# Another order of the slots of an expert's block over the partitions

## What is computed

```python
def hier_moe(h, p):
    """h (N, D): top-1 expert group, then top-2 experts inside it; experts are SwiGLU MLPs."""
    ...
    order = jnp.argsort(e_assign)
    e_s, tok_s, w_s = e_assign[order], tok_assign[order], w_assign[order]
    ...
    buf = jnp.zeros((n_blocks * EXPERT_BLOCK, D_MODEL), h.dtype).at[dest].set(h[tok_s])
    ...
    def expert_block(args):
        xb, e = args
        return (jax.nn.silu(xb @ p['w_exp_gate'][e]) * (xb @ p['w_exp_up'][e])) @ p['w_exp_down'][e]

    out = lax.map(expert_block, (buf.reshape(n_blocks, EXPERT_BLOCK, D_MODEL), block_expert))
    out = out.reshape(-1, D_MODEL)
    return jnp.zeros((n, D_MODEL), h.dtype).at[tok_s].add(out[dest] * w_s[:, None].astype(h.dtype))
```

## Time and profile before

| what | value |
|---|---|
| median of three timed executions | 1260.64 us |
| the profiled execution, its own time | 1264.99 us |
| its span, first to last instruction | 1263.3 us |
| TensorE busy in the span | 1041.9 us (82%) |
| VectorE, ScalarE, GpSimd busy | 410.2, 328.0, 251.9 us |
| weights of the experts | 192 pieces of 1 MB |
| gathers and scatters of 4 KB rows | 34 gathers, 32 scatters |
| stretch with the DMA engines at or above 0.9 | slices 25 to 38 of 40, 758 to 1200 us |

### The profile page before, as it was taken

How to read it: one execution, slowest core, us unless ns; L and a number is a source line. 1 busy time by engine, 2 the same in 40 slices (tenths; PEclk the granted TensorE clock), 3 DMA queues, 4 the chain that set the end, 5 groups by cost and what they waited for, 6 DMA issues and landing times.

```text
span 1263.3 us, 17373 instructions
## 1 busy us (share of the span) xinstructions
PE 1041.9 (82%) x6707; PEld 662.2 (52%) x6707; DVE 410.2 (32%) x917; ACT 328.0 (26%) x666; POOL 251.9 (20%) x551
## 2 busy tenths in 40 slices
PE   5999999779987776989999589987877788888870
PEld 5999999656665553767644333333332333333320
DVE  4346536646844443422413520100000000000006
ACT  6432221445642222120011112322222122211222
POOL 0005960388832110000000001111110111111010
PEclk9999999887978887989999679999899999998895
DMA  8322334331017542770220869999999999999956
GB/s 341 138 68 70 108 120 163 104 149 34 2 38 255 181 134 90 315 275 1 76 123 17 322 254 402 390 401 415 403 405 398 406 402 403 405 407 410 405 228 229
DMA packets 74993, 299.64 MB, mean 237 GB/s; under 512 B 12471, under 2 KB 34871, under 8 KB 48407
## 3 DMA queue, kind: packets, MB, share of 16 engines
q1 hardware_dynamic: 65854, 279.89, 57.5%
q0 software_dynamic: 7904, 17.59, 4.3%
q10 hardware_dynamic: 1152, 1.05, 0.3%
HBM read 284.26 MB, written 25.05 MB: 245 GB/s over the span
## 4 chain that ended last, share of the span: by engine, by line
DMA 27%; PE 25%; DVE 3%; issue 2%; SPq 2%; ACT 1%; POOL 0%; POOLq 0%
DMA local_tail<-in_w_exp 14%; DMA arena<-in_w_exp 11%; PE ps L2199 6%; PE ps L1779 5%; PE ps L1739 3%; PE ps L1700 3%; PE ps L1749 2%; PE ps L2216 2%; SPq L2108 1%; PE ps L2186 1%; PE ps L1716 1%; DVE arena L2358 1%; PE ps L1711 1%; SPq L2113 1%; DMA arena<-scratch_h,arena 1%
## 5 line engine op out<-in xcount | busy, mean ns | idle before, releaser
L352 PE MATMUL ps<-local_project 128*128 128x288 f32 (+4 forms) x1608 | 207.2, 291 | 15.3 <-DVE local_project L490 11.6
L2199 PE MATMUL ps<-arena,local_tail 128*64 128x512 f32 x760 | 196.7, 607 | 27.7 <-DMA arena<-in_w_exp 20.3
L352 PEld LDWEIGHTS ps<-local_project 128*128 128x128 f32 (+1 forms) x1608 | 205.8, 185 | 16.3 <-DVE local_project L391 11.5
L2301 DVE SCALAR_TENSOR_TENSOR local_tail<-arena,ps 64x512 f32<-64x512 f32 x32 | 21.7, 679 | 427.4 <-ACT arena L2267 427.4
L2199 PEld LDWEIGHTS ps<-arena,local_tail 128*64 128x64 f32 x760 | 63.2, 139 | 133.7 <-issue 132.1
L2216 PE MATMUL ps<-arena 128*64 128x512 f32 x256 | 89.3, 679 | 32.4 <-DMA arena<-in_w_exp 15.6
L2144 POOL DMA_INDIRECT scratch_rows<-local_tail,arena x32 | 29.5, 922 | 394.3 <-ACT local_tail L2275 393.2
L2216 PE MATMUL ps<-local_tail,arena 128*64 128x512 f32 x256 | 89.6, 681 | 16.1 <-DMA local_tail<-in_w_exp 16.1
L2199 PE MATMUL ps<-local_tail 128*64 128x512 f32 x264 | 80.1, 596 | 5.3 <-DMA local_tail<-in_w_exp 4.2
L2275 ACT ACTIVATE local_tail<-ps 64x512 f32<-64x512 f32 x64 | 37.9, 593 | 148.4 <-PE ps L2216 147.6
L2216 PEld LDWEIGHTS ps<-arena 128*64 128x64 f32 x256 | 26.4, 155 | 76.9 <-issue 73.5
(11 more groups left out here) (401 smaller groups left out, 1505.7 us busy)
## 6 DMA issues: line engine op xcount, KB each, us to landing
arena<-in_w_exp SPq DMA_DIRECT2D x127, 1024.0 KB, 29.0
local_tail<-in_w_exp SPq DMA_DIRECT2D x65, 1024.0 KB, 29.4
arena<-in_w_rest SPq DMA_DIRECT2D x9, 1024.0 KB, 5.6
local_attention<-in_cache SPq DMA_DIRECT2D x56, 128.0 KB, 2.7
arena<-in_w_wide SPq DMA_DIRECT2D x6, 1040.0 KB, 4.9
arena<-scratch_sig SPq DMA_DIRECT2D x2, 2304.0 KB, 13.4
arena<-in_x SPq DMA_DIRECT2D x2, 2048.0 KB, 11.7
arena<-in_cache SPq DMA_DIRECT2D x32, 128.0 KB, 2.2
```

The source lines that it names most:

```text
L352: mm = pe.matmul(out, stationary(s, k), moving(m, k), start=k == 0 and a == 0, stop=k == KD - 1 and a == 2)
L2199: mm = pe.matmul(c.ps[SLOTS * u:SLOTS * (u + 1), BANKS[q][u], :], XT[:, 4 * half + k], c.sets[s][2 * half + u][:, k], start=half == 0 and ...
```

## The change

One constant is made in another way. Before, slot (partition) p took the token of rank p. Now partition p takes the token of rank 16 (p mod 4) + p / 4 (whole division). Partitions 0 to 7 so hold ranks 0, 16, 32, 48, 1, 17, 33, 49. The constant feeds the table and the short way of the first two blocks alike, so gathers, products and scatters agree. No instruction is added, removed or moved on any engine: each engine's list of instructions is the same in both kernels. What differs is which partitions hold a token when fewer than 64 do.

```diff
@@ -119,7 +119,7 @@
     c["valid"][:] = np.arange(TILES) * P + r[:, None] < TOK
     c["blkno"][:] = np.arange(BLOCKS)
     c["blkslot"][:] = SLOTS * np.arange(TABLE + 1)
-    c["slot"][:] = np.arange(SLOTS) - SLOTS
+    c["slot"][:] = np.arange(SLOTS) % 4 * 16 + np.arange(SLOTS) // 4 - SLOTS
 
     token = np.arange(TILES)[None, None, :, None] * P + r[:, None, None, None]
```

## The result

The changed kernel takes 1275.11 us in the median of four timed executions (1272.44 to 1276.52), the kernel before, timed beside it, 1261.41 us. The ratio is **1.0091, with a 95% interval of 1.0058 to 1.0123**: slower, by 13.7 us in the medians, by 11.5 us in the ratio, and by 7 to 16 us within its interval. Forecast were 22.4 us. The profiled execution of after took 1272.44 us with a span of 1270.7 us, 7.45 us more than the profiled execution before.

What follows compares the result with a forecast made beforehand. The weight stream bounds the kernel from about 820 us, its end set by the last DMA engine. Terms 21.8 + 0.3 + 0.3 = 22.4 us, on the median of 1260.64 us, gave 1283.0 us, range 1270 to 1289 us.

Steps and rivals of the forecast that it cites:

- So I take engine = partition mod 16: Gathers and scatters: rows are dealt one to each of 16 DMA engines, then again, read from the last scatter's rounds.
- The count of rows: Rows beside the weight stream: the worst engine goes from 165 to 240, 75 rows more.
- The price of a row: Time one 4 KB row adds to its DMA engine beside the weights: 0.29 us, with ends 0.16 and 0.33.
- the taper: End of the weight stream before: the share falls evenly, last engine 17 us after the first, read as 56 rows' difference.
- the main term: Worst DMA engine's extra rows delay the last weight landing: 75 x 0.29 = 21.8 us (12.0 to 24.8).
- The two small terms: First gather gets a fourth row on its worst engine, last scatter a fourth round: 0.3 us each.
- The forecast's cover for the other scatters: Scatters land in 11.5 us against 16 us for a block; a fourth row's 0.3 us is hidden by waiting for weights.
- The other signs: Profile after: two blocks take 33.9 to 34.5 us, GB/s falls to about 385 and the DMA share below 1.
- The second step, to 0.25 or less: End of the weight stream: after a step to some 0.5, the share drops to 0.25 or less and holds to the end.
- It levels the engines: Rival: dealing is by neighbouring partitions, so the new order evens the engines; 7 us earlier, 1253.6 us; chance 0.05.
- nothing moves: Rival: dealing turns between groups of 16 partitions, worst engine 159 rows before and after; 1260.6 us; chance 0.05.
- The bare price: Rival: a row beside the weights costs only 0.16 us, sum 12.0 + 0.5, 1273 us (1270 to 1277); chance 0.18.

Runs made afterwards that it cites:

- ranks dealt over pairs: Kernel before, with partition p holding rank 16 (2 (p / 32) + p mod 2) + (p / 2) mod 16: 1256.06 us, ratio 0.9958.
- offsets: Kernel before, with each expert from the third on starting at another slot, 5e mod 16, and two more VectorE instructions: 1260.29 us, ratio 0.9992.
- both halves: Kernel before, reordered so each round of 16 ranks lies in 32 partitions, not 16 neighbouring ones: 1261.87 us, ratio 1.0001.
- pairs, offsets: Kernel with ranks dealt over pairs, plus another starting slot (5e mod 16) for each expert from the third on: 1256.54 us, ratio 0.9956.
- both halves, offsets: Kernel with rounds of 16 ranks spread over 32 partitions, plus another starting slot for each expert from the third on: 1258.55 us, ratio 0.9969.
- one engine: Kernel before, with only ranks 32 and 48 exchanged for ranks 14 and 15, loading one engine by partition mod 16: 1267.85 us, ratio 1.0041.
- groups exchanged: Kernel before, with the second and third group of 16 ranks changing places: 1274.7 us, ratio 1.0113.

## Why the prediction was right and where it failed

**Right: the bound and the sign.** The last DMA engine sets the end of the weight stream, the new order gives eight engines nearly all rows, and the stream ends later. The step to a share of 0.5 at 1216 us is the sign that was named for it. Everything ahead of the experts stayed. In part this was luck: the new order splits the engines eight and eight by partition mod 16 (206 to 240 rows against 2 to 95) and by pairs (217 to 234 against 26 to 65) alike, so the sign and the step came out though the dealing was wrong. The time lies in the stated range, 1270 to 1289 us, but in the part that the forecast gave to a rival (1270 to 1277 us): the width of the range holds it, not the working behind 1283 us.

**The step that failed: "So I take engine = partition mod 16".** It was read from the rounds of the lone scatter, taken as 16, 16 and 5 rows. These rounds exclude groups of four neighbours, the one dealing by neighbours that I held against them. But the last five were read from one window of 0.5 us, and that window hides two rounds. Cut finer, in the kernel before:

```profile
1232.90:1233.00 0.10, 0.00 (x0) 0.00 (x0) 0.00 (x0) 0.00 (x0) 0.00 (x0) 0.50 0.27 41
1233.00:1233.10 0.10, 0.00 (x0) 0.00 (x0) 0.00 (x0) 0.00 (x0) 0.00 (x0) 0.50 0.33 42
1233.10:1233.20 0.10, 0.00 (x0) 0.00 (x0) 0.00 (x0) 0.00 (x0) 0.00 (x0) 0.50 0.02 0
1233.20:1233.40 0.20, 0.00 (x0) 0.00 (x0) 0.00 (x0) 0.00 (x0) 0.00 (x0) 0.50 0.18 41
```

That is one row, one row, a gap, and two more rows. With 33 rows ahead of them, the rounds are 16, 16, 3 and 2. By partition mod 16 no engine has a fourth row. By pairs partitions 32 to 36 lie on three engines that have two rows already: two of them get a third and a fourth row and one a third, which is 16, 16, 3 and 2. So the trace of before already told the two dealings apart; the joined window didn't. The second support, that 165 down to 109 rows fit an even taper, doesn't tell them apart either: by pairs the engines have 192, 180, 171, 163, 160, 150, 138 and so on down to 88, even too. The Trainium skill, "DMA: Bandwidth & Descriptors", section "The descriptor swizzle", gives an engine four neighbouring partitions and the four that lie 32 further on, for a transfer to 128 partitions. The measured rule for these DMAs of 64 has the same form with two in place of four. The prediction took the page's groups of four as the only form of neighbours, and so put aside with them what was nearly right.

**The count of rows.** By pairs the fullest engine goes from 192 to 234 rows, 42 more, not 75 (165 to 240).

**The price of a row.** 0.29 us was the taper of 17 us over 56 rows. By pairs there are 104 rows between the first engine and the last, and 17 / 104 = 0.16 us, the bound from below: the time that 4.1 KB takes at 25.6 GB/s. Other orders say the same: in the trace the sixteen landings of the last weight piece lie 17.1 us apart in before, 9.6 us with ranks dealt over pairs, 8.8 us with offsets and 7.9 us with both halves. By pairs that is over 104, 56, 46 and 46 rows, 0.16 to 0.19 us a row; by partition mod 16 it would be over 56, 82, 10 and 56. (Levelled further, 19 and 10 rows leave 5.0 and 3.9 us, so some 2 us of a fall don't come from rows.) So the main term, 75 x 0.29 = 21.8 us, is 42 x 0.16 = 6.7 us. Both factors came from one wrong rule, and both were too large by about 1.8. Put shortly, the forecast scaled the 17 us of the taper by 75 / 56, and the right counts scale it by 42 / 104, to 6.9 us.

The nine orders with all their work, side by side (fullest engine by pairs, what 0.16 us a row makes of its difference from before, the change of the experts' stretch in the profile, the timed ratio):

| order | rows | x 0.16 us | stretch, us | ratio |
|---|---|---|---|---|
| pairs, offsets | 141 | -8.2 | -5.7 | 0.9956 |
| both halves, offsets | 146 | -7.4 | -4.2 | 0.9969 |
| offsets | 160 | -5.1 | -3.4 | 0.9992 |
| both halves | 161 | -5.0 | -3.0 | 1.0001 |
| pairs | 165 | -4.3 | -3.1 | 0.9958 |
| before | 192 | 0 | 0 | 1 |
| one engine | 213 | +3.4 | +4.2 | 1.0041 |
| after (two profiles) | 234 | +6.7 | +8.2, +7.7 | 1.0091, 1.0099 |
| groups exchanged | 240 | +7.7 | +13.4 | 1.0113 |

A straight line through the stretches of these nine kernels has 0.17 us for a row, one through the timed ratios 0.19 us. The counts by partition mod 16 don't order the table at all: 165 rows (both halves, before, groups exchanged) stand at -3.0, at 0 and at +13.4 us, and 240 (one engine, after) at +4.2 and at +8.

**What stays open in size.** The stretch explains 8 us of after's loss, and the ratios stand for 11.5 and 12.5 us. Their intervals begin at 7 and 8 us, so the two needn't differ; with four timed runs behind each ratio I can't say whether a few us more are lost. The exchanged groups cost 6 us more than their rows, and the kernel before lies 2 us below the line. Equal rows didn't give equal times either: both halves and pairs have 161 and 165, and 1.0001 and 0.9958. The fullest engine's rows are the main cause, not the whole.

**The two small terms** (0.3 us each, for a fourth row in the first gather and the last scatter) didn't come: the first gather was on the chain for 7.41 us in place of 7.99 and the last scatter for 2.68 in place of 3.10. (The forecast's cover for the other scatters, 11.5 us, is from a view that mixes them with the loads of `scratch_rows`; the scatters alone land in at most 8.2 us, and the argument stands.) The lone scatter did go half as wide, as forecast, but not slower; by pairs it had four rounds before too. Its windows in after:

```profile
1239.90:1240.20 0.30, 0.00 (x0) 0.00 (x0) 0.00 (x0) 0.00 (x0) 0.00 (x0) 1.00 0.72 178
1240.20:1240.50 0.30, 0.00 (x0) 0.00 (x0) 0.00 (x0) 0.00 (x0) 0.00 (x0) 1.00 0.56 205
1240.50:1240.80 0.30, 0.00 (x0) 0.00 (x0) 0.00 (x0) 0.00 (x0) 0.00 (x0) 1.00 0.31 123
```

All 37 rows move within 0.9 us, four on an engine: a round takes 0.2 us here, not the 0.3 of the earlier trace rows. That 0.3 was the second support of the price, and it was no fixed price of a row either: with four rows on the fullest engine each time, a round takes 0.3 us in the kernel before and with exchanged groups, and 0.2 us here. Why it differs wasn't separated.

**The other signs.** Two blocks take 33.3 us, more than before but less than the 33.9 to 34.5 named; GB/s falls to 400 and not to 385, and the share stays at 1.01 until 1200 us. A difference of 234 - 26 rows between engines is 33 us at 0.16, about the 29.7 us that a piece is in the queue, so by this count the engines with few rows run ahead and lack work only near the end. The second step, to 0.25 or less, isn't there: by pairs the eight full engines have 217 to 234 rows and end within 3 us, as the window from 1231 us shows.

**The rivals.** "It levels the engines" and "nothing moves" fell. "The bare price" (1273 us) comes nearest to the measured time, and has the right price, but with 75 rows: its 12 us are made of a right factor and a wrong one, and that they are near the timed loss proves nothing for it.

## What to carry to other kernels

Where several transfer engines share one load, level the rows on them by the rule that an experiment shows, since the fullest engine sets the end: here one constant is worth 0.4% one way and 0.9% the other. Before a count is built on a rule of dealing, write down what every other simple rule would show in the same rows, cut the windows until each holds one round, and exchange two groups that the rule calls equal: if the time moves, the rule is wrong. When a price and a count come from one assumption, an error in it enters the sum twice.

## What the runs showed of the hardware

- The indirect gathers and scatters of 64 rows of 4 KB here give a DMA engine two neighbouring partitions and the two that lie 32 further on. For scatters the rounds of the lone one show it: 16, 16, 3 and 2 rows in before, 11, 10, 8 and 8 with exchanged groups. For gathers it follows from the times: the new order costs 3.8 us of the stretch with scatters alone and about 8 us with both, and dealing over pairs gains 0.4%.
- Beside a stream that keeps the engines at a share of 1, a row costs the engine that carries it 0.16 to 0.17 us, its bytes at the stream's rate.
- A gathered row costs the stream more than that. Half of the gathered rows are some 33 on an engine, 5.3 us at 0.16, but leaving them out shortened the stretch by 12.3 us; without any the stream runs at 420 GB/s and not 405. Whether the slots read their own rows of `h` or all read one row made no difference (0.6 us).
